# Two narrower matmul widths for the experts, and the choice of width made in one hub with the transposes behind it

## What is computed

```python
def moe_swiglu(h, w_router, b_router, w1, w3, w2):
    logits = h.astype(jnp.float32) @ w_router.astype(jnp.float32) + b_router.astype(jnp.float32)
    top_v, top_i = lax.top_k(logits, TOP_K)          # 2 of 8
    gates = jax.nn.softmax(top_v, axis=-1)
    comb = jnp.sum(jax.nn.one_hot(top_i, N_EXPERTS, dtype=jnp.float32) * gates[..., None], axis=-2)
    ...
    for e in range(N_EXPERTS):
        y = y + comb[..., e:e + 1] * swiglu(h, w1[e], w3[e], w2[e])   # 1024 -> 1408 -> 1024
    return y
```

## Time and profile before

| what | value |
|---|---|
| median of the timed runs | 1675.71 us |
| the profiled execution | 1675.75 us, span 1674.0 us |
| experts' stage, first to last matmul of the experts | 1033.7 to about 1629 us |
| TensorE busy | 92% of the span |
| widths that ran, experts 0 to 7 | 144, 144, 144, 144, 144, 208, 160, 144 |
| mean granted clock of TensorE | 0.971 |

### The profile page before, as it was taken

The page is one execution under the profiler, slowest core; times in us unless marked ns, Lnnn a source line. Parts: engine busy times, 40 slices in busy tenths (PEclk is TensorE's granted clock), DMA queues, the critical chain, the costliest instruction groups (busy, mean ns, idle before and its releaser), DMA issues.

```text
span 1674.0 us, 26732 instructions
## 1 busy us (share of the span) xinstructions
PE 1548.1 (92%) x11956; PEld 1463.9 (87%) x11956; DVE 477.0 (28%) x804; ACT 371.9 (22%) x622; POOL 416.6 (25%) x224
## 2 busy tenths in 40 slices
PE   7699989999999999999998975999999998999992
PEld 4399879899999999998997954999999988999992
DVE  1457662500111011226986231011110110010115
ACT  2321252322221222223225221111111110010114
POOL 0358135332343334424923302000000000000005
PEclk9899999999999999999999997999999998999995
DMA  7646242554343332333534083879789793748644
GB/s 234 190 130 174 76 126 82 176 168 127 86 124 119 101 101 61 104 125 104 156 97 126 6 288 128 274 272 323 244 270 330 271 306 117 247 151 303 221 140 176
DMA packets 291576, 286.76 MB, mean 171 GB/s; under 512 B 8109, under 2 KB 283199, under 8 KB 291414
## 3 DMA queue, kind: packets, MB, share of 16 engines
q1 hardware_dynamic: 203286, 230.23, 41.8%
q10 hardware_dynamic: 84400, 42.51, 9.2%
q0 software_dynamic: 3760, 12.09, 1.9%
HBM read 266.45 MB, written 19.07 MB: 171 GB/s over the span
## 4 chain that ended last, share of the span: by engine, by line
PE 87%; DVE 5%; DMA 3%; SPq 2%; issue 2%; ACT 1%; POOL 1%; POOLq 0%; ACTq 0%; DVEq 0%
PE PP L783 36%; PE PP L1109 22%; PE PP L1121 11%; PE PP L824 7%; PE PP L796 3%; PE PP L757 2%; PE PP L768 1%; DMA adaw<-in_w_ada 1%; PE PP L1080 1%; PE PP L1091 1%; DVE mem L1584 1%; DVE mem_r L1578 1%; PE PP L957 1%; DMA mem<-in_w_ada 1%; SPq L508 1%
## 5 line engine op out<-in xcount | busy, mean ns | idle before, releaser
L783 PE MATMUL PP<-hT_r,mem_r 128*128 128x260 f32 x2624 | 435.4, 285 | 4.6 <-DVE xT L1596 3.2
L639 POOL TENSOR_TENSOR mem_r<-mem,mem_r 128x1024 fp32r<-128x1024 f32 (+1 forms) x108 | 317.8, 2959 | 471.6 <-ACT mem_r L1237 471.2
L1109 PE MATMUL PP<-big,mem 128*128 128x144 f32 (+2 forms) x2816 | 375.2, 296 | 13.2 <-issue 12.4
L1109 PEld LDWEIGHTS PP<-big,mem 128*128 128x128 f32 x2816 | 372.9, 192 | 14.1 <-issue 12.8
L783 PEld LDWEIGHTS PP<-hT_r,mem_r 128*128 128x128 f32 x2624 | 363.7, 188 | 11.6 <-issue 7.7
L783 PE MATMUL PP<-mem_r 128*128 128x260 f32 x1312 | 263.8, 283 | 0.0
L783 PEld LDWEIGHTS PP<-mem_r 128*128 128x128 f32 x1312 | 201.8, 188 | 0.0
L1121 PE MATMUL PP<-big,mem 128*128 128x144 f32 (+2 forms) x1408 | 193.5, 294 | 0.0
L1121 PEld LDWEIGHTS PP<-big,mem 128*128 128x128 f32 x1408 | 186.6, 190 | 0.0
L739 POOL DMA_INDIRECT mem<-y_by_expert,place x10 | 9.5, 949 | 617.2 <-SPq L586 614.4
L824 PE MATMUL PP<-adaw,cs 128*9 128x128 f32 x1280 | 148.3, 274 | 14.0 <-DMA adaw<-in_w_ada 9.1
(11 more groups left out here) (237 smaller groups left out, 1064.9 us busy)
## 6 DMA issues: line engine op xcount, KB each, us to landing
mem<-in_w_moe SPq DMA_DIRECT2D x48, 1536.0 KB, 8.7
mem<-in_w_moe SPq DMA_DIRECT2D x32, 1408.0 KB, 8.8
adaw<-in_w_ada ACTq DMA_DIRECT2D x80, 512.0 KB, 5.0
mem<-in_w_dense SPq DMA_DIRECT2D x20, 1024.0 KB, 5.4
mem<-in_w_in SPq DMA_DIRECT2D x16, 1024.0 KB, 5.6
mem<-in_w_moe SPq DMA_DIRECT2D x16, 1024.0 KB, 7.0
mem<-in_w_dense SPq DMA_DIRECT2D x16, 704.0 KB, 4.7
mem<-in_w_out SPq DMA_DIRECT2D x8, 1024.0 KB, 5.1
```

What stands on the lines that cost most here:

```text
L639: pool.tensor_tensor(r_(raw), raw, read_(hi), ALU.subtract).then_inc(w_lo, 1)
L783: mm = pe.matmul(PP[q][:, h, 0:HT], r_(w[:, k, :]), r_(x[:, k, HT * h:HT * h + HT]), start=(i == 0 and w is wh and x is hi), stop=(i == le ...
L1109: mm = pe.matmul(PP[w][:, f % 2, 0:n], raw[:, w, k, :], hn[:, k, 0:n], start=(k == 0), stop=(k == KD - 1))
```

## The change

`WIDTHS` becomes 128, 136, 144, 160, 176, 208, 256. For each expert the compares come first, all in one place, the hub. Behind them stand seven short stretches, one for each width (`between`). A stretch places a hint, transposes the next rows (`rows_tr` for t = 0 and 1, 16 transposes) and the second half of the last expert's result (`y_tr` for j = 4 to 7, 8 transposes), and ends with the jump to the block of its width. The seven blocks (`expert`) stand behind the hub. A block holds the steps f and q and `y_tr` for j = 0 to 3, and closes with the hinted jump to the next hub, now in the widest block too. ScalarE's and VectorE's copies move accordingly: the rows for the next expert are copied when the steps q are over, and `y_rows(e, 1)` comes right behind them.

```diff
-WIDTHS = [144, 160, 176, 208, NW]
+WIDTHS = [128, 136, 144, 160, 176, 208, NW]
@@ TensorE
                     mm.then_inc(R["f_done"], 1)
-                    if f == 1 and e:
-                        y_tr(e - 1, KD - 1)
...
                     mm.then_inc(R["y_done"], 1)
-                    if q:
+                    if 1 <= q <= 4:
                         y_tr(e, q - 1)
-                    if q in (3, 5) and e + 1 < NE:
-                        rows_tr(e + 1, (q - 3) // 2)
-                    if q == 3 and n < NW:
+                    if q == 3:
                         over = pe.mark_branch_hint_location()
-                if n < NW:
-                    pe.br_lt(c, T + 1, on_true=f"expert_over{e}", on_false=f"expert_over{e}").branch_hint(over)
-                else:
-                    pe.br(f"expert_over{e}")
+                pe.br_lt(c, T + 1, on_true=f"expert_over{e}", on_false=f"expert_over{e}").branch_hint(over)
+
+            def between(e, n, c):
+
+                ahead = pe.mark_branch_hint_location()
+                for t in range(2):
+                    rows_tr(e, t)
+                if e:
+                    for j in range(4, KD):
+                        y_tr(e - 1, j)
+                pe.br_lt(c, T + 1, on_true=f"expert{e}_block{n}", on_false=f"expert{e}_block{n}").branch_hint(ahead)
...
                 if len(widths) == 1:
-                    expert(e, n, c)
+                    between(e, n, c)
...
                 with nc.body(f"expert{e}_of_{n}", valid_engines=[pe.engine]):
-                    expert(e, n, c)
+                    between(e, n, c)
...
-            for t in range(2):
-                rows_tr(0, t)
             for e in range(NE):
                 by_width(e, counts[e], WIDTHS)
+                for n in WIDTHS:
+                    with nc.body(f"expert{e}_block{n}", valid_engines=[pe.engine]):
+                        expert(e, n, counts[e])
                 nc.switch_bb(f"expert_over{e}")
-            y_tr(NE - 1, KD - 1)
+            for j in range(4, KD):
+                y_tr(NE - 1, j)
@@ ScalarE
-                    if e + 1 < NE:
-                        if q in (3, 5):
-                            rows_odd(e + 1, (q - 3) // 2)
+                if e + 1 < NE:
+                    for t in range(2):
+                        rows_odd(e + 1, t)
@@ VectorE
-                    if e and f == 1:
-                        y_rows(e - 1, 1)
-                if e + 1 < NE:
-                    rows_even(e + 1, 0)
                 if e:
                     dve.wait_ge(R["y_out"], 32 * e)
                 y_rows(e, 0)
                 if e + 1 < NE:
-                    rows_even(e + 1, 1)
-            y_rows(NE - 1, 1)
+                    for t in range(2):
+                        rows_even(e + 1, t)
+                y_rows(e, 1)
```

## The result

The changed kernel takes 1685.9 us (median of 9 runs) against 1675.7 before; the ratio is 1.0061, with a 95% interval of 1.0037 to 1.0085. In a second measurement it took 1687.0, ratio 1.0075 (1.0042 to 1.0107). The forecast was 1669.0 and faster.

What follows compares the result with a forecast made beforehand. Bound: number of passes times pitch, plus two idle pieces at TensorE. 1675.75 - 42.4 (narrower passes, old entries) + 35.4 (seven new entries) + 0.3 = 1669.0 us; range 1640 to 1693, the forecast's own 1656 to 1679.

Steps and rivals of the forecast that it cites:

- tail: At the very end of the kernel, three more parts are turned behind the last step q: 0.3 us added.
- Pitch: Experts' passes: time follows a straight line in columns, 0.1089 us at 128, 0.1156 at 136; gain 28.3 us.
- rival with a floor of 0.12: Passes of 128 and 136 columns run at 0.12 us because loading weights limits; gain 6, time 1691; chance 0.08.
- The old entries: Entries of experts 5 and 6 lose 12.4 us of idle time; with 1.7 us of lower clock, 14.1 together.
- the light ones: New entries of experts 1, 2 and 7, stretch in the hub's first piece of instructions: 3.0 us each.
- The heavy ones: New entries of experts 3 to 6, waiting before and behind the transposes: 4.9 us, plus 1.7 for the clock, each.
- The clock: Entries of experts 3 to 6: only transposes run, which don't count as busy TensorE, so 1.7 us each.
- Why a hint in the stretch doesn't help: Hint heads 24 transposes lasting 2.6 us, mostly too late to help; each entry costs at least 2.55 us.
- The second piece of the hub: For experts 3 to 6 the stretch is fetched only on arrival: one wait before the transposes, one behind.
- What is hidden: Copies of hn covered to 0.1 us, else 0.9 us per expert; `y_rows`, SyncE's waits and weights cause no delay.
- half-way rival: Entries from expert 1 on cost 1 to 2.5 us each, giving 1644 to 1655; chance 0.15.
- slower rival: Hub entries cost what expert 5's did, four at 9.83 + 1.7, three at 5: 1695; chance 0.22, including all above 1679.

Runs made afterwards that it cites:

- the version with direct jumps: Against the kernel before: seven widths, no hub, old transpose places, early compare and hint, jumps straight from block to block; 1635.2 us, ratio 0.9775.
- the kernel with the widths alone: The kernel before with only the seven widths, compares and transposes in their old places; 1669.2 us, ratio 0.9962.
- the hub without stretch: The changed kernel with transposes and copies back in their old places, only hint and jump behind each compare; 1678.3 us, ratio 1.0028 to before.
- the version without hints: The version with direct jumps, its early compares kept but no hint for the jump into the next block; 1681.0 us, ratio 1.0040 to before.

## Why the prediction was wrong

The stage was to become 6.7 us shorter (28.3 and 14.1 off, 35.4 and 0.3 on) and became 5.6 longer in the first profile and 11.6 in the second. With "busy at full clock" from the version with direct jumps (555.5 us for the same 4464 matmuls and transposes, at a clock of 1.00), the changed kernel's stage splits into 555.5 + 34.1 idle + 12.3 at the lower clock (18.3 in the second profile); the stage before, 24.0 us wider passes, into 579.5 + 12.6 + 4.2. The step that failed is the price of the seven entries: 35.4 us in the prediction (28.6 idle, 6.8 at the lower clock), 46.3 and 52.4 in the two profiles. Term by term:

| term | predicted | first profile | second |
|---|---|---|---|
| widths | -28.3 | -24.0 | -24.0 |
| idle time by issue, old entries off, new on | -12.4 + 28.6 | +21.5 | +21.5 |
| passes and transposes at the lower clock | -1.7 + 6.8 | +8.1 | +14.1 |
| tail | +0.3 | in the above | in the above |
| sum | -6.7 | +5.6 | +11.6 |

- **What bounds the kernel**: right. Number of passes times pitch, plus idle time by issue; nothing else appeared.
- **Pitch**: right in kind at 136, where the line said 0.1156 and 22 passes of the version with direct jumps take 1157.54 - 1154.99 = 2.55 us, 0.116. Too low at 128: 0.1089 by the line, 2.45 / 22 = 0.111 in the trace. That is the floor of the earlier trace rows, 0.11, which the prediction had named and not taken. Measured, the widths give 3 x 528 x (0.1223 - 0.1114) + 2 x 528 x (0.1223 - 0.1159) = 24.0 us. The rival with a floor of 0.12 did not happen.
- **The old entries**: right, they are gone, 12.4 us; experts 5 and 6 pay the new price instead.
- **Idle time of the new entries**: the first term that was too small, 28.6 for 34.0. "Each entry is at least expert 6's case, 2.55 us", taken at 3.0 for the light ones, where experts 2 and 6 show 3.59 and 3.99, and expert 7 only 0.7. The heavy ones, taken at 4.9, were to be experts 3 to 6; they are 1, 3, 4 and 5, with 6.8, 6.8, 6.0 and 6.2. Of jumps with a single stop the trace of before held one, and it was at the cheap end: the same kind of jump costs 5.19 us in the kernel with the widths alone and 5.17 in the hub without stretch.
- **The clock**: the second term, 6.8 predicted at the entries against 12.3 in the first profile and 18.3 in the second (the 2.5 us of expert 0's cold start, within the 4.2 of before, occurred in neither). The prediction charged 1.7 us to four entries. Single stops can bring it too (expert 6's 3.99 us in both profiles, expert 2's 3.97 in the second), and the transposes are stretched as well, expert 3's to 3.67 us from 1.91. The earlier trace rows had the price of one such fall; the number of them was wrong. The row from 1029 to 1033 also didn't bear what was read from it on transposes: in the changed kernel's first profile TensorE waits 17.0 us, runs 16 transposes and nothing else from 1033.55, and the clock reads 0.50 up to 1035.5, 0.73 up to 1037.0 and 1.00 from there, ahead of the first f matmul at 1037.67. It rose on transposes alone. What the prediction cites from the Trainium skill ("TensorE: Matmul & The Clock Gate", Part 4) and this measurement differ, and the measurement decides.
- **Why a hint in the stretch doesn't help**: right. Without it the kernel is only 9.5 us slower and most of that at one entry; given 240 passes ahead, a hint is worth 6.5 us an entry. The Trainium skill ("Runtime: NRT & Kernel Launch", Instruction fetch mechanics) has a taken branch to a page that isn't at hand force a fetch before execution goes on; the version without hints agrees, with 30.1 us of idle time by issue over its seven entries. With the early hint the same jumps cost 2.5.
- **The second piece of the hub**: stops ahead of the transposes came, at experts 3, 4 and 5 as foreseen, but at 1 too and not at 6; where the pieces begin, no run shows. It was wrong as the main cause of the loss: with the hub cut to some 75 instructions 9 of the 11 us saved ahead of and inside the transposes came back behind them.
- **What is hidden**: right. The copies of hn, `y_rows`, SyncE's waits and the weights never showed.
- **Chances**: the entries came to 34.0 + 12.3 = 46.3 us in the first profile and 34.1 + 18.3 = 52.4 in the second, and the prediction itself had put the turning point at 42.7 (by its own terms 42.4 less the tail of 0.3, 42.1; its half-way rival comes to 1641 to 1651 by the same terms and its 3 to 6 us an entry to 1655 to 1676, which changes nothing here). With the widths at 24.0 in place of 28.3 it lay lower still. The outcome lies between its forecast and its slower rival (1695), in the part above 1679 that had 0.22. A better value was in its rows: the two entries of before cost 2.55 and 9.83 + 1.7 us, 7.0 on average, or 49 for seven; it took 5.1 each.

## What to carry to other kernels

Where a kernel picks one of several long unrolled blocks at run time, the price is in the jump: 6.5 us each here (some 4 idle, the rest half-clock passes behind it), unless a hint for the very jump that will be taken stands far ahead of it (240 passes, some 30 us, here), and then next to nothing. So decide early: compare, hint, work on, and jump straight to the target, without a hub that has to be loaded itself. Only then do finer variants pay, and before adding them look at the floor of a pass, here 0.111 us at 128 columns and 0.110 at 96.

## What the runs showed of the hardware that I had not expected

- A jump without an early hint can stop TensorE twice, at the target and a few passes behind it (3.28 and 4.24 us). With a hint 2.7 us ahead four entries stopped once (1.66 to 2.67 us), two twice and one not at all.
- With one early hint one entry in seven still stopped with seven widths (expert 7's, 1.21 us), three with nine; with two hints none at the jump, and one. The versions differ in where blocks and hints lie in the program; what decides it wasn't tested.
- The length of a stop alone doesn't tell what the clock does: 3.59 us at expert 2's entry left it at 1.00 in one execution of the changed kernel and 3.97 us there were followed by 0.51 in another, while 2.54 us at expert 5's entry without hints were followed by 0.50 from 1394 to 1397.
- The experts' stage began at 1029.6 to 1039.0 us over 16 profiled executions, a spread larger than several of the effects studied here. A spread of 6.6 us is there by the 501st matmul, so most of it arises long before the code that the versions change.
